# The start of a decoder-layer kernel in another order: first key scores in two halves, two attention rounds later, output products by head group

## What is computed

```python
def _mixer(x, mem_k, mem_v, lru_buf, h0, sc_buf, lp):
    proj = jnp.einsum('bsd,de->bse', x, lp['w_in'])
    ...
    y_lru = h.astype(x.dtype) * jax.nn.gelu(gate, approximate=False)
    ...
    y_sc = sc_b * u
    ...
    y_mem = jnp.einsum('bhsm,bmhd->bshd', p, mem_v).reshape(bsz, s, D_MEM)
    y = jnp.concatenate([_rmsnorm(y_lru, lp['g_lru']), _rmsnorm(y_sc, lp['g_sc']), _rmsnorm(y_mem, lp['g_mem'])], axis=-1)
    out = jnp.einsum('bse,ed->bsd', y, lp['w_out'])
...
def _peer(x, wq, keys, u_tab, v_tab):
        qb = jnp.einsum('td,de->te', xb, wq).reshape(PEER_BLOCK, PEER_HEADS, 2, PEER_DK // 2)
        sk = jnp.einsum('thpd,hpkd->thpk', qb, keys).astype(jnp.float32)
        v1, i1 = lax.top_k(sk[:, :, 0], PEER_TOPK)
        v2, i2 = lax.top_k(sk[:, :, 1], PEER_TOPK)
        ...
        g = jax.nn.softmax(top_s, axis=-1).astype(xb.dtype)
        act = jax.nn.gelu(jnp.einsum('td,thkd->thk', xb, u_tab[e]), approximate=False)
        return jnp.einsum('thk,thkd->td', g * act, v_tab[e])
```

## Time and profile before

| | us |
|---|---|
| median of 3 runs | 3128.4 |
| the runs | 3127.5, 3134.21, 3128.4 |
| the profiled execution | 3130.84 |
| its span (first to last instruction) | 3129.0 |

### The profile page before, as it was taken

The page is one execution under the profiler, slowest core; times in us unless marked ns, Lnnn a source line. Parts: engine busy times, 40 slices in busy tenths (PEclk is TensorE's granted clock), DMA queues, the critical chain, the costliest instruction groups (busy, mean ns, idle before and its releaser), DMA issues.

```text
span 3129.0 us, 36184 instructions
## 1 busy us (share of the span) xinstructions
PE 2483.7 (79%) x10228; PEld 733.3 (23%) x10228; DVE 2150.1 (69%) x4941; ACT 1400.3 (45%) x4040; POOL 1231.7 (39%) x1092
## 2 busy tenths in 40 slices
PE   9989988889886998888878879866666766666676
PEld 5633322222221332223322213311111111100010
DVE  3675778888756577887776686676667666764554
ACT  2335455555445343554544353443334444433343
POOL 0034544454444444444334334343444343443342
PEclk9999999999897998989989979967777677776777
DMA  5369999999999999999999999999999999999997
GB/s 217 133 258 416 405 417 416 390 409 420 420 421 415 418 420 418 413 402 401 420 420 415 420 374 420 420 422 421 421 421 416 421 410 421 409 422 421 421 405 319
DMA packets 186889, 1239.60 MB, mean 396 GB/s; under 512 B 21056, under 2 KB 24384, under 8 KB 46528
## 3 DMA queue, kind: packets, MB, share of 16 engines
q0 software_dynamic: 156672, 1140.92, 88.5%
q1 hardware_dynamic: 29872, 95.84, 8.0%
...
## 4 chain that ended last, share of the span: by engine, by line
issue 49%; POOL 33%; PE 8%; DMA 7%; DVE 1%; ACT 1%; POOLq 0%; SPq 0%; DVEq 0%; ACTq 0%
POOL arena L706 33%; DMA arena<-in_uv,idxT 7%; PE ps L733 2%; PE ps L1002 1%; PE ps L863 1%; PE ps L984 1%; DVE arena L1654 1%; PE ps L913 0%; POOLq L698 0%; PE ps L943 0%; PE ps L753 0%; DMA consts<-in_consts 0%; PE ps L769 0%; PE ps L797 0%; ACT wset L1234 0%
## 5 line engine op out<-in xcount | busy, mean ns | idle before, releaser
L706 POOL DMA_INDIRECT arena<-in_uv,idxT x1088 | 1231.5, 1132 | 1869.0 <-PE ps L1002 1618.7
L1654 DVE CUSTOM_DVE_ANT_0 arena<-arena 128x1024 f32<-128x1024 f32 x1088 | 1326.5, 1223 | 788.8 <-DMA arena<-in_uv,idxT 716.5
L1002 PE MATMUL ps<-arena,wset 128*32 128x512 f32 x4352 | 1370.7, 735 | 616.5 <-ACT wset L1234 614.2
L1225 ACT ACTIVATE gel<-acts 128x1 f32<-128x1 f32 x1088 | 219.1, 201 | 1292.3 <-DVE acts L1654 1290.3
L1002 PEld LDWEIGHTS ps<-arena,wset 128*32 128x32 f32 x4352 | 174.1, 118 | 1516.6 <-ACT wset L1234 1340.4
L1229 ACT ACTIVATE wt<-gel,gT 128x1 f32<-128x1 f32 x1088 | 320.5, 295 | 103.4 <-ACT gel L1225 3.7
L1234 ACT ACTIVATE wset<-arena,wt 128x32 f32<-128x32 f32 x1088 | 349.5, 321 | 36.1
L733 PE MATMUL ps<-arena 128*128 128x384 f32 (+1 forms) x768 | 308.0, 522 | 6.5 <-DMA arena<-in_xT 6.5
L913 PE MATMUL ps<-arena 128*128 128x384 f32 (+3 forms) x896 | 289.6, 452 | 0.7 <-DVE small L1430 0.7
L984 PE MATMUL ps<-arena 32*128 32x512 f32 x704 | 236.1, 752 | 3.2 <-ACT arena L1204 3.0
L913 PEld LDWEIGHTS ps<-arena 128*128 128x128 f32 x896 | 148.2, 193 | 199.7 <-issue 155.8
...
## 6 DMA issues: line engine op xcount, KB each, us to landing
...
arena<-in_uv,idxT POOLq DMA_INDIRECT x1088, 15.7
...
```

Of the source, the lines that this page charges most:

```text
L706: pool.indirect_dma_start(out=ring[n % RING], out_offset=None, in_=A["uv"], in_offset=bass.IndirectOffsetOnAxis(ap=idxT[t % 2][:, col:col ...
L1002: last = mm(ps[r0:r0 + 32, hf * HALF:(hf + 1) * HALF], wset[n % SETS][:, :], v[:, hf * HALF:(hf + 1) * HALF], start=first, stop=final)
L1225: A_(gel[:, n % COLS:n % COLS + 1], acts[:, n % COLS:n % COLS + 1], ACT.Gelu).then_inc(gelus, 1)
L1654: V.tensor_tensor_reduce(out=ring[n % RING][:, 0:D], in0=ring[n % RING][:, 0:D], in1=xrep[g % 2], scale=1.0, scalar=0.0, op0=ALU.mult, op1 ...
```

## The change

The steps of attention rounds 4 and 5, the memory group's RMSNorm of tokens 128 to 383 and all that depends on them go from before slot 0 into slots 0 to 5 (of rounds 4 and 5 the scores, maximum, exponential and division stay before it, now behind the first routing). The four query sides `w0` 0 to 3 follow each other with only `Ka`, the key scores of sides 0 and 1, between them; `Kb` does sides 2 and 3, in bank 0. DVE's route for unit 0 has four pieces in place of three. `op` (1,0) and (2,0) are split: `pa` (LRU, four k blocks) and `pm` (short convolution, two) stay before slot 0, `pb` (memory, two) goes to slot 5; `op` (1,1) and (2,1) move from slots 3 and 7 to 6 and 9, and are spread in four pieces of two k blocks with pace 0.5. Gather 6 waits for `pm` (2,0). One block of output weights moves from ring buffer 7 to `x1b[1]`. Banks are given out anew. The steps of tile 1's LayerNorm come two slots later.

```diff
-    as.3 nm.2.1 xt.0.0 xt.0.1 w0.0 w0.1 at.3 w0.2 av.3 as.4 w0.3 as.5 K0.0 at.4 w0.4 av.4 at.5 w0.5 av.5 R0
-    w0.6 nm.0.1 w0.7 S0.0 K0.1 op.1.0 op.2.0
+    as.3 nm.2.1 xt.0.0 xt.0.1 w0.0 w0.1 Ka.0 w0.2 w0.3 Kb.0 at.3 w0.4 av.3 as.4 w0.5 R0 w0.6 w0.7 S0.0 K0.1
+    as.5 pa.1.0 pm.1.0 pa.2.0 pm.2.0
...
-    sq.2.1 sq.5.1 sq.3.1 tc.2 dv.0 rm.1.1 rm.2.1 xe.0.0 xe.0.1 ex.3 tc.3 w0.0 w0.1 w0.2 ex.4 w0.3 tc.4 ex.5
-    tc.5 w0.4 sq.6.1 w0.5 sq.7.1 E0.0 w0.6 rm.0.1 C0 w0.7 G0.0
+    sq.2.1 sq.5.1 sq.3.1 tc.2 dv.0 rm.1.1 rm.2.1 xe.0.0 xe.0.1 ex.3 w0.0 w0.1 w0.2 w0.3 tc.3 w0.4 w0.5 C0
+    w0.6 E0.0 w0.7 G0.0 ex.4 ex.5
...
-    l2.0.1 ty.2 mx.3 nz.3 no.1.1 no.2.1 ty.3 mx.4 nz.4 mx.5 T0.0.0 ty.4 nz.5 T0.0.1 ty.5 T0.0.2 I0.0 no.0.1
-    T0.1.0
+    l2.0.1 ty.2 mx.3 no.1.1 nz.3 T0.0.0 no.2.1 T0.0.1 T0.0.2 T0.0.3 ty.3 I0.0 mx.4 mx.5 T0.1.0 nz.4 nz.5
     """
...
+    put("pe", 0, 0, "at", 4)
+    put("act", 0, 0, "tc", 4)
+    put("pe", 0.5, 0, "at", 5)
+    put("act", 0.5, 0, "tc", 5)
+    put("pe", 1, 0, "av", 4)
+    put("dve", 1, 0, "ty", 4)
+    put("pe", 1.5, 0, "av", 5)
+    put("dve", 2, 0, "ty", 5)
+    put("act", 2, 0, "sq", (6, 1))
+    put("act", 2, 0, "sq", (7, 1))
+    put("pe", 3, 0, "nm", (G_MEM, 1))
+    put("act", 3, 0, "rm", (G_MEM, 1))
+    put("dve", 4, 0, "no", (G_MEM, 1))
+    put("pe", 5, 0, "pb", (1, 0))
+    put("pe", 5, 0, "pb", (2, 0))
     put("dve", 0, 0, "T0", (1, 1))
     put("act", 1, 0, "E0", 1)
-    put("dve", 1, 0, "z", (1, 0))
-    put("dve", 2, 0, "z", (2, 0))
-    put("pe", 3, 0, "op", (1, 1))
+    put("dve", 6, 0, "z", (1, 0))
+    put("dve", 7, 0, "z", (2, 0))
+    put("pe", 6, 0, "op", (1, 1))
     put("dve", 3, 0, "T0", (1, 2))
     put("pe", 5, 0, "S0", 1)
     put("dve", 6, 0, "I0", 1)
     put("act", 7, 0, "G0", 1)
-    put("dve", 6, 0, "z", (1, 1))
-    put("pe", 7, 0, "op", (2, 1))
-    put("dve", 10, 0, "z", (2, 1))
+    put("dve", 8, 0, "z", (1, 1))
+    put("pe", 9, 0, "op", (2, 1))
+    put("dve", 11, 0, "z", (2, 1))
     for ti in (1, 2):
-        x = (7, 12)[ti - 1]
+        x = (9, 12)[ti - 1]
         plan_norm(0, ti, x)
         for hh in range(2):
             put("pe", x + 8 - ti + hh, 0, "xt", (ti, hh))
...
-PE_PACE = {"half": 0.5, "oq": 1, "wq": 0.5, "w0": 0.25, "wa": 0.33, "xt": 0.25, "nm": 0.25, "ss": 0.25, "sv": 0.25}
+PE_PACE = {"half": 0.5, "op": 0.5, "oq": 1, "wq": 0.5, "w0": 0.25, "wa": 0.33, "xt": 0.25, "nm": 0.25, "ss": 0.25, "sv": 0.25}
...
-    w_out = [ring[RING - 2][:, 0:D], ring[RING - 2][:, D:], ring[RING - 1][:, 0:D], ring[RING - 1][:, D:],
+    w_out = [ring[RING - 2][:, 0:D], ring[RING - 2][:, D:], ring[RING - 1][:, 0:D], x1b[1],
...
+    scores = {u: [bank[1] if u == 1 else bank[0] if u == 0 and si >= 2 else kbank for si in range(4)]
+              for u in range(NUNIT)}
...
     def abank(b, r_):
 
-        return 1 if b == 0 and r_ % 2 else MB[2]
-
-    def nbank(b, g):
-        return 0 if b == 0 else MB[2] if g == G_MEM else MB[1]
+        return (3 if r_ == 5 else 1) if b == 0 and r_ % 2 else MB[2]
+
+    def obank(ti, half):
+        return MB[(half, 1 - half, half)[ti]]
+
+    def wbank(name, side):
+        return MB[(0, 1, 2, 0, 1, 0, 1, 0)[side] if name == "w0" else side % 3]
+
+    def nbank(b, g, part):
+        return (MB[2] if (g, part) == (G_MEM, 1) else 0) if b == 0 else MB[2] if g == G_MEM else MB[1]
...
             if n == RING - 2:
-                after(pool, "pe", 0, "op", (2, 0))
+                after(pool, "pe", 0, "pm", (2, 0))
...
+                if (b, arg) == (0, 5):
+                    pe.wait_ge(idx_ready, 1)
+                    pe.wait_ge(gT_ready, 1)
...
-            elif name in ("op", "oa", "ob"):
+            elif name in ("op", "oa", "ob", "pa", "pm", "pb"):
                 ti, half = arg
-                ks = GROUPS[G_LRU][1] + GROUPS[G_MEM][1] + GROUPS[G_SC][1]
-                ks = {"op": ks, "oa": ks[:6], "ob": ks[6:]}[name]
-                k_ = MB[(2 * ti + half) % 3]
-                o_ = bank[k_] if name == "ob" else claim(k_, "dve", b, "z", arg)
+                lru, mem, sc = GROUPS[G_LRU][1], GROUPS[G_MEM][1], GROUPS[G_SC][1]
+                every = lru + mem + sc if ti == 0 else lru + sc + mem
+                ks = {"op": every, "oa": lru + mem, "ob": sc, "pa": lru, "pm": sc, "pb": mem}[name]
+                k_ = obank(ti, half)
+                o_ = claim(k_, "dve", b, "z", arg) if name in ("op", "oa", "pa") else bank[k_]
                 if name == "oa":
                     pe.wait_ge(ld["wout"], 16 * KD)
-                    after(pe, "dve", b, "no", (G_LRU, 0))
-                    after(pe, "dve", b, "no", (G_MEM, 0))
-                elif name == "ob":
-                    after(pe, "dve", b, "no", (G_SC, 0))
-                else:
-                    for g in range(3):
-                        after(pe, "dve", b, "no", (g, 1))
-                for k in ks:
+                for g in {"oa": (G_LRU, G_MEM), "ob": (G_SC,), "pa": (G_LRU,), "pm": (G_SC,), "pb": (G_MEM,),
+                          "op": (0, 1, 2)}[name]:
+                    after(pe, "dve", b, "no", (g, 0 if ti == 0 else 1))
+                for i, k in enumerate(ks):
                     w_ = w_out[4 * half + k // 2][:, (k % 2) * HALF:(k % 2 + 1) * HALF]
-                    last = mm(o_, x8(zone2, b)[:, k, ti * P:(ti + 1) * P], w_, start=k == 0, stop=k == 5)
-                last.then_inc(stage["pe"], 1)
-                yield
+                    last = mm(o_, x8(zone2, b)[:, k, ti * P:(ti + 1) * P], w_, start=k == every[0], stop=k == every[-1])
+                    if i == len(ks) - 1:
+                        last.then_inc(stage["pe"], 1)
+                    if i % 2:
+                        yield
...
+        def first_scores(part):
+
+            after(pe, "act", 0, "w0", 2 * part + 1)
+            if part:
+                after(pe, *holder[0])
+            else:
+                pe.wait_ge(ld["keys"], 16)
+            for si in (2 * part, 2 * part + 1):
+                last = mm(scores[0][si][:, si * NK:(si + 1) * NK], q_of(0, 0)[:, si * P:(si + 1) * P],
+                          keysT[:, si * NK:(si + 1) * NK], start=True, stop=True)
+            last.then_inc((k_first, k_mm)[part], 1)
...
             if u == 1:
                 after(pe, *holder[1])
-            elif u:
+            else:
                 pe.wait_ge(idx_ready, u)
                 pe.wait_ge(gT_ready, u)
...
+                after(pe, "dve", 0, "ty", 5)
...
+                if b == 0:
+                    after(act, "pe", b, "pb", (2, 0))
...
+                after(dve, "pe", b, "ob" if ti == 0 else "op" if half else "pb", arg)
+                o_ = bank[obank(ti, half)]
...
-                for _ in range((8, 6, 4)[part]):
+                for _ in range(((4, 4, 6, 4), (8, 6, 4))[u_][part]):
...
-            dve.wait_ge(k_mm, u + 1)
+            dve.wait_ge(k_mm if u else k_first, u + 1)
             for si in range(4):
-                for _ in top16(scr[:, 0:NK], scores[u][:, si * NK:(si + 1) * NK], val[:, si * TOPK:(si + 1) * TOPK],
+                if u == 0 and si == 2:
+                    dve.wait_ge(k_mm, 1)
```

More of the change, by code:

```diff
@@ L458, in build @@
     kbank, xr, ybank = bank[3], ps[:, 6 * 512:8 * 512], ps[:, 0:D]
-    scores = {u: bank[1] if u == 1 else kbank for u in range(NUNIT)}
+    scores = {u: [bank[1] if u == 1 else bank[0] if u == 0 and si >= 2 else kbank for si in range(4)]
+              for u in range(NUNIT)}
     ld = {k: sem("ld_" + k) for k in ("consts", "par", "cvst", "scst", "wrg", "memT", "wkv", "ln", "ln2", "wout", "keys",
@@ L942, in keyscores @@
                 if t < TILES:
-                    last = mm(scores[u][:, si * NK:(si + 1) * NK], q_of(t, k)[:, si * P:(si + 1) * P], keysT[:, a_:a_ + NK],
+                    last = mm(scores[u][si][:, si * NK:(si + 1) * NK], q_of(t, k)[:, si * P:(si + 1) * P], keysT[:, a_:a_ + NK],
                               start=True, stop=True)
@@ L947, in keyscores @@
                         b_ = a_ + half * PH * NK
-                        last = mm(scores[u][half * NS:(half + 1) * NS, si * NK:(si + 1) * NK],
+                        last = mm(scores[u][si][half * NS:(half + 1) * NS, si * NK:(si + 1) * NK],
                                   q_of(t, k + 2 * half)[:, si * NS:(si + 1) * NS], keysT[:, b_:b_ + NK],
@@ L1133, in run @@
                 lo, hi = span(b, part)
-                ins = A_(rmsbuf[g][:, lo:hi], bank[nbank(b, g)][:, 0:hi - lo], ACT.Sqrt,
+                ins = A_(rmsbuf[g][:, lo:hi], bank[nbank(b, g, part)][:, 0:hi - lo], ACT.Sqrt,
                          scale=1.0 / GROUPS[g][2], bias=eps[:, 0:1])
@@ L1154, in run @@
                 after(act, "pe", b, "w0", arg)
-                ins = A_(q_of(0, k)[:, si * P:(si + 1) * P], bank[MB[arg % 3]][:, 0:P], ACT.Copy)
+                ins = A_(q_of(0, k)[:, si * P:(si + 1) * P], bank[wbank("w0", arg)][:, 0:P], ACT.Copy)
             elif name in ("wa", "we"):
@@ L1481, in run @@
                 dve.wait_ge(ld_zx[ti], 16)
```

(4 more changed lines are left out.)

15 lines of the change are left out of this document (9 added, 6 removed).

## The result

| | before | after |
|---|---|---|
| median, us | 3132.66 (5 runs, 3127.5 to 3134.21) | 3149.06 (5 runs, 3147.63 to 3152.2) |
| ratio to before | 1 | 1.0055 [1.0044, 1.0066] |
| profiled execution, its span | 3130.84, 3129.0 | 3149.37, 3147.6 |
| combine 21 starts | 256.31 | 273.18 |

The new kernel is slower by 0.55%, outside the predicted range of 3121 to 3142. By gather number, the issue in after less that in before is -8.2 us at gather 0, -11.2 at 12, +4.6 at 14, +9.9 at 20, +16.9 at 28, and from there it stays between 15.9 and 17.7 us at the gathers read (+17.7 at gather 1080). Gather n waits for combine n - 8 (n from 8 on), so it turns between combine 4, which releases the buffer of gather 12, and combine 20, which releases that of gather 28; the head start of 11.2 us is spent there too, on the products that after still owes.

A forecast was written before the change was run, and what follows sets the result against it. PE, never idle from 251 to 397 us, was taken to pace the slots. PE 8.2 us later at slot 21, less 1.7 held by the queue, gave +6.5 on 3128.4: 3135 us, range 3121 to 3142.

The forecast's parts named there:

- the walk: Step-by-step times from 141.8 us: `select` at 166.1, combine 0 at 183.4, combine 4 at 199.4, combine 21 at about 264.7.
- it does not do what it says: Rival, chance 0.06: side 3's weights or the second half's scores come late, route 1 to 3 us later; 3137.
- the two new waits: Slots 5 to 11: PE waits 3.1 us ahead of `pb` (1,0) for `no`, 3.3 ahead of `op` (1,1) for `z`.
- I take the same loss in both kernels: PE's loss to a lower clock is equal before and after: 0 us of change, bounded at 6 less or more.
- the clock: Rival, chance 0.12: four new PE idles each followed by some 2 us at half rate, half on the path; +4, 3139.
- Spreading `op` in pieces evens the gathers, but takes nothing from PE's sum: Slots 5 to 11: splitting `op` between combines leaves PE's total work the same, 0 us.
- the ledger: Up to combine 21 the shift is the change of PE's idle and clock: idle 27 against 18.7, 8.2 us later.
- The 2 us for tile 1's table loads: Slots 12 to 21: 2 us of PE idle added for tile 1's `dv`, a table load each way, and two `l2`.
- the 1.2 for combine 12: Slots 12 to 21: 1.2 us of PE idle added because combine 12 waits for `z` (2,1).
- less the 1.7 us that the queue held: Behind slot 21: queued gather work absorbs 1.7 us of PE's 8.2 us delay, leaving +6.5 at the end.
- wrong if the landings stay at 8 us with a later combine 21: Sign against the forecast, for gathers issued around 310 us; it expected landings near 6.2 us between 300 and 340.
- gaps from the DMA share: From 176 to 251 us, share 0.88 leaves 9 us of DMA gaps, the most a head start could gain.

The follow-up runs named there:

- a3: The changed kernel with filler products that nothing reads in five of PE's idles up to `op` (1,1), all waits kept; median 3140.5 us, ratio 1.0031.
- a4: The changed kernel with both new waits taken away and filler products ahead of `select` and in slots 1 and 4; median 3136.75 us, ratio 1.0020.
- c2: c1 with four filler products added ahead of the first `select`; median 3130.25 us, ratio to before 1.0000.
- a5: The changed kernel with `op` (1,1) and (2,1) in one piece each (pace 0), not spread; median 3145.99 us, ratio 1.0050.
- b2: The kernel before with six products that nothing reads (5.3 us of PE) in slot 20, just ahead of combine 20; ratio 1.0029.
- c1: The changed kernel's early routing, with attention 4 and 5, memory norm and `pb` back before slot 0, `op`, `z`, norms in old slots; median 3135.53 us, ratio 1.0015.
- b1: The kernel before with filler products in three PE gaps: ahead of round 5's transposes, ahead of `op` (1,0), and in slot 1; ratio 0.9995.

## Why the prediction was right or wrong

The forecast was +6.5 us, and the medians show +16.4, the spans +18.6. Of the 14 us between the forecast 3135 and the measured 3149.06, 4.3 us are the base alone: the prediction counted from 3128.4, the median of three runs, and five runs of before gave 3132.66.

**Right: the walk.** The steps fell where they were put, each a little late: `select` at 166.40 (forecast 166.1) after an idle of 3.89 (3.7); the first L706, now L727, at 167.98 (167 to 168):

```profile
167.98 1.08 POOL L727 DMA_INDIRECT arena<-in_uv,idxT  x1 [167.53 <-DVE idxT L1631]
...
184.94 0.94 POOL L727 DMA_INDIRECT arena<-in_uv,idxT  x1 [9.67 <-PE ps L884]
```

The seventh gather, at 184.94, missed its 181 to 183: `pa` and `pm` took 12.78 us, partly at the lower clock, not 12 x 0.89 and 1 us. Combines 0 and 4 came at 185.74 and 201.27 (183.4 and 199.4). The weights of side 3 caused no wait, so the rival *it does not do what it says* falls.

**Right: the two new waits.** `pb` waited 1.83 us from 202.3 to 204.16 (3.1, to 203.5), and `op` (1,1) 3.31 us to 216.76 (3.3, to 214.9), each ended by the closing signal of a DVE step (L1332). Both waits were forecast, and the first was over-sized by 1.3 us.

**Wrong: "I take the same loss in both kernels" (the clock).** This term was set to 0 and bounded at 6 us; it measured 11.1 us (16.9 for 5.8). The rival *the clock* had the right kind, four idles each followed by half rate, but priced them at 4 us together, took no other stretch in, and so gave 3139. Three of its four idles were followed by lower clock directly (3.89, 1.83 and 3.31 us), and the stretch that cost most, 15.0 us of busy time from 247.6 to 264.6 us, stood behind short idles that it did not list. a3, a4 and c2 show the mechanism: with idles filled the lower clock costs 5.8 and 1.7 us for 16.9, and 8.2 for 10.7, and the medians of a3 and c2 fall by 8.6 and 5.3 us against the same kernel without fillers. The Trainium skill (TensorE: Matmul & The Clock Gate, HAM oscillation) warns of idle gaps that send the clock back again and again; the trace agrees, with four stretches at 0.50 in 131 us, where I had kept that rule out of the sum.

**Wrong: "Spreading `op` in pieces evens the gathers, but takes nothing from PE's sum".** This term was put at nothing, and the ledger's opening sentence, that the shift is the change of idle time and of clock, rests on it. It measured 3.0 us: 92.8 us at full clock for 89.8, since combines that follow each other directly run in pairs and spread ones do not. a5 gives the 3.0 us back in that column, though not in its time.

**Mis-sized: the idle.** The ledger had 27 for 18.7, +8.2. Measured: 21.5 for 18.7, +2.8. Up to combine 11 the new idles summed to 15.2 (16.9 forecast) and before's were 13.3, not 12.1; from combine 11 to 21 idle was 6.3 (10 forecast) where before's was 5.4, not 6.6. The 2 us for tile 1's table loads and the 1.2 for combine 12 did not show as that much more idle. On a table load the trace keeps to the earlier trace rows: 1.28 us (the row below, of after, just ahead of slot 0's gelu). The next activation starts at 183.28, 1.29 us after the load does, so that no further drain shows. What a switch costs otherwise was not tried by itself.

```profile
181.99 1.28 ACT L1265 ACT_TABLE_LOAD   x1 [8.54 <-DVE acts L1696]
```

**Wrong: "less the 1.7 us that the queue held".** The landings of after's gathers issued in 305:315, not near 6.2:

```profile
DMA to landing us min/median/max: 7.9/8.6/9.1
```

The shift of after did not shrink behind slot 28; b2 shows the same for a delay alone, in its trace and in its median (+6.4 us for a filler of 5.3). Other traces are less steady: c1's shift went from 7.7 us at gather 100 to 3.9 at gather 200, and b1's from -1.4 to -5.5, with a mean clock in between of 0.98 and 0.96 for 0.94 in before. So one trace cannot settle 1.7 us; but after's 18.6 at the end for 16.9 at combine 21, and b2's median, speak against it. This was the case named as *wrong if the landings stay at 8 us with a later combine 21*. A gather is issued when a combine releases its buffer, so with a later PE the issue is later too, and landing less issue says nothing of how much a later PE may cost. Up to 397 us PE of before is never idle, and so has nothing to make a delay good with; behind that PE has idle time (88.97 us busy of the 103 from 397 to 500), while the DMA share is 1.02 there, and full DMA engines cannot make good what they did not move before. By the windows' GB/s before had moved 146 x 34 + 339 x 75 + 411 x 146 = 90.4 MB from 142 to 397 us and after 206 x 34 + 267 x 75 + 385 x 146 = 83.2. The 7.2 MB are 17 us at the 420 GB/s of the later slices of the page: the whole loss. That the DMA engines are what keeps the delay is argued from these figures; no run tests it by itself.

**A step that was not put to the test: gaps from the DMA share.** The 9 us that I gave as the most that a head start could gain came from the share of 0.88. By bytes, 339 of 420 GB/s over 75 us, it would be 14.5 us. No kernel gained enough to tell.

The sum again, with what was measured: 2.8 of idle, 11.1 of clock, 3.0 of combines that no longer pair, nothing off, gives 16.9 at combine 21; the span grew by 18.6. What the last 1 to 2 us of the span are was not looked for.
